# Next block's Q projection and rope tables inside the current attention loop, in a two-layer decoder trunk

## The chip, the cores and the metric

The kernel runs on the eight cores of one Trainium2 chip. Each core computes one of the eight sequences of the batch; the cores exchange nothing. The metric is the device time of the slowest core, in microseconds.

## The reference

Two layers over x of 2048 tokens by 1024 features per core. Each layer first mixes tokens, then runs an MLP:

```python
h = adaln(rms_norm(x, g_mix), sh1, sc1)
q_a,k_a,v_a, q_b,k_b,v_b, gate_a, gate_b = split(h @ w_in)
# A: sliding window 128, 8 query heads, 2 key heads, a learned sink per head
# B: 8 heads, blocks of 256 keys: own block (causal) + the top 3 past blocks by q . mean(k)
q, k = rope(rms_norm(q), positions), rope(rms_norm(k), positions)   # head size 64
y_a = swa_attention(q_a, k_a, v_a, sinks) @ w_o_swa
y_b = moba_attention(q_b, k_b, v_b) @ w_o_moba
x = x + gt1 * ((sigmoid(gate_a) * y_a + sigmoid(gate_b) * y_b) @ w_out)
h = adaln(rms_norm(x, g_mlp), sh2, sc2)
x = x + gt2 * (relu(h @ w_up) ** 2 @ w_down)
```

## The kernel before

Activations are held with features on the partitions. The 2048 tokens are cut into NS = 4 blocks of 512 (index `s`). A small scheduler records every operation in program order with what it reads and writes, derives the semaphores from that, and lets each engine run its own operations in exactly that order. All helpers (`mm`, `act`, `tt`, `ts`, `stt`, `cp`) have one line each, so that in the profile L373 is every matmul, L398 every ScalarE activation, L402, L416 and L428 are VectorE operations, L435 copies.

A layer runs: the keys and values of all tokens (A); then for each block the Q projection, the bias of the block selection, and attention (B0 to B3); then the output projections (C) and the MLP. The change is in B.

- `norm_tile(s, ..., hTs)` normalises block `s` into `hTs`: eight squares on ACT with eight matmuls into one PSUM bank, Ln and Exp, and eight pairs of a DVE operation and an ACT Identity. The bank is the next of `gen_banks`.
- `rope_tables(s)` makes cos and sin of the block: ten DVE operations, then two Sin activations on ACT, which have another activation table than Exp, Ln and Square.
- `qk_item` makes one item (128 of the 1024 Q features) out of three parts. `s0` projects: eight matmuls into `pin`. `s1` squares `pin` on ACT, averages over the head with one matmul into `pm`, runs Ln and Exp on ACT and multiplies `pin` by the result on DVE. `s2` rotates: one matmul into `pr`, and three DVE operations that end in `AT`, which holds Q and later the attention result. `pin` rotates over PSUM banks 0 to 2, `pm` is bank 3, `pr` banks 4 and 5. Two sets of scratch tiles (`qksets`) alternate.
- `run_items` runs eight items in ten steps; step i issues `s0` of item i, then `s1` of item i-1, then `s2` of item i-2. In step 7 `norm_tile(s+1)` stands behind the last projection. `rope_tables(s+1)` follows the ten steps.
- The bias stage works mostly on DVE, with one transpose on PE for each 128 tokens.
- The attention loop runs over `units`. A unit is one tile of 128 keys for up to 512 query columns and has four parts: `score` (matmuls into a score bank `sc`, with a POOL copy of the values and for some units DVE copies of Q), `ex` (one Exp on ACT into a probability tile `pb`), `pv` (one matmul into `po`), and `post`, which for the last unit of a group runs Ln and Exp on ACT and the products on DVE. First come 14 or 16 units of the sliding window (attention A), then eight heads of 4s + 4 units each (attention B, called the MoBA part below): 46, 80, 112 and 144 units for s = 0 to 3. `score` is issued SK = 3 units ahead of `ex` and `pv`, `post` two units behind. Scores rotate over banks 1 to 4, probabilities over four tiles, `po` over banks 5 to 7. For s of 2 and 3 most units have an extra matmul for the bias.

Of the kernel before, what the change touches and what calls it, by code (L numbers as in the profile page):

```python
# [6 lines left out]
F32 = mybir.dt.float32  # L7
BF16 = mybir.dt.bfloat16
# [8 lines left out]
NS = 4  # L17
# [278 lines left out]
def build_program(layers, n_total_layers=2, dbg=None, stop=None):  # L296
    nc = bass.Bass("TRN2", target_bir_lowering=False)
    L = n_total_layers
# [16 lines left out]
    S = Sched()  # L315
    dbg_out = {}
    with ExitStack() as st:
        XA = Arena(nc, st, "XA", 65536, gran=2048)
        AA = Arena(nc, st, "AA", 32768, gran=1024)
        BIG = Arena(nc, st, "BIG", 65536, gran=256)  # L320
# [3 lines left out]
        SF2 = Arena(nc, st, "SF2", 4096, gran=1024)  # L324
# [3 lines left out]
        PS = [PsumBank(nc, st, "ps%d" % i) for i in range(8)]  # L328

        xT = XA.view(0, (8, SEQ), F32)  # L330
        AT = AA.view(0, (8, SEQ), BF16)
# [37 lines left out]
        def mm(out, lhsT, rhs, start, stop):  # L369
            r = list(lhsT.keys) + list(rhs.keys)  # L370
            if not start:
                r += list(out.keys)
            S.add('pe', lambda e, o=out.ap, l=lhsT.ap, rr=rhs.ap: e.matmul(o, l, rr, start=start, stop=stop),  # L373
                  reads=r, writes=out.keys)
# [65 lines left out]
        def memset(out, val, eng='dve'):  # L440
            S.add(eng, lambda e, o=out.ap: e.memset(o, val), writes=out.keys)
# [112 lines left out]
        def GAIN(l, i):  # L554
            return vec(l, 0, 68)[:, 64 + i:65 + i]

        def norm_tile(s, acol, bcol, dest):
            sl = slice(s * 512, (s + 1) * 512)
            bank = psb()
            pm = bank.view(0, (512,), F32)  # L560
            for k in range(8):
                act(dest[:, k], xT[:, k, sl], AF.Square)
                mm(pm, Oones, dest[:, k], start=(k == 0), stop=(k == 7))
            act(rstd, pm, AF.Ln, bias=epsc)
            act(rstd, rstd, AF.Exp, scale=-0.5)
            for k in range(8):
                stt(t1 if k % 2 == 0 else t2, xT[:, k, sl], acol[:, k:k + 1], rstd, ALU.mult, ALU.mult)
                act(dest[:, k], t1 if k % 2 == 0 else t2, AF.Identity, bias=bcol[:, k:k + 1])
# [3 lines left out]
        qkc = [0]  # L572
        pinc = [0]
        qkn = [2]

        def qk_item(proj, gain, dest, cs=None):
            st_ = {}

            def s0():
                st_['pin'] = PS[pinc[0] % 3].view(0, (512,), F32)  # L580
                pinc[0] += 1
                st_['set'] = qksets[qkc[0] % qkn[0]]
                qkc[0] += 1
                proj(st_['pin'])

            def s1():
                sq_, xn_, r_, tt1_ = st_['set']
                pin = st_['pin']
                act(sq_, pin, AF.Square)
                pm = PS[3].view(0, (512,), F32)  # L590
                mm(pm, Bones, sq_, True, True)
                act(r_, pm, AF.Ln, bias=epsc)
                act(r_, r_, AF.Exp, scale=-0.5)
                stt(xn_, pin, gain, r_, ALU.mult, ALU.mult)

            def s2():
                sq_, xn_, r_, tt1_ = st_['set']
                pr = PS[4 + st_.setdefault('prb', qkc[0] % 2)].view(0, (512,), F32)
                mm(pr, Rt, xn_, True, True)
                cos_, sin_ = cs if cs is not None else (cos_s, sin_s)  # L600
                tt(tt1_, xn_, cos_, ALU.mult)
                tt(r_, pr, sin_, ALU.mult)
                tt(dest, tt1_, r_, ALU.add)
            return (s0, s1, s2)

        def run_items(items, fillers=None, after_proj=None, mid=None):
            n = len(items)
            for i in range(n + 2):
                if i == 3 and mid is not None:
                    mid()  # L610
                if fillers:
                    fillers.pop(0)()
                if i < n:
                    items[i][0]()
                if i == n - 1 and after_proj is not None:
                    after_proj()
                if 0 <= i - 1 < n and items[i - 1][1] is not None:
                    items[i - 1][1]()
                if 0 <= i - 2 < n and items[i - 2][2] is not None:
                    items[i - 2][2]()  # L620

        BIGROW = 32768
        AAROW = 16384
# [7 lines left out]
        def layer(l):  # L631
# [112 lines left out]
            biasq3 = SB.view(13312, (8, 8), BF16)  # L744
            E_GS = 1024 // 4
            VECROWF = 1024
            Pb3 = [Pb[0], Pb[1], BIG.view(63744, (512,), BF16), SF2.view(0, (512,), BF16)]
            vaug = [BIG.view(64768 + 256 * i_, (128,), BF16) for i_ in range(3)] + [SB.view(15616, (128,), BF16)]
            for i_ in range(4):
                memset(vaug[i_][:, 64:128], 1.0)  # L750
            norm_tile(0, a1, sh1, hTs)
            rope_tables(0)
            for s in range(NS):
                gen_banks[0] = [6, 7]
                S.mark('L%d B%d qproj' % (l, s))
                sl = slice(s * 512, (s + 1) * 512)
                def mk_q(p):
                    w = wqa if p < 4 else wqb
                    pc = p % 4

                    def proj(pin):
                        for k in range(8):
                            mm(pin, w[:, k, pc * 128:(pc + 1) * 128], hTs[:, k], k == 0, k == 7)
                    return qk_item(proj, GAIN(l, 0 if p < 4 else 2), AT[:, p, sl])
                run_items([mk_q(p) for p in range(8)],
                          after_proj=(lambda s=s: norm_tile(s + 1, a1, sh1, hTs)) if s + 1 < NS else None)
                if s + 1 < NS:
                    rope_tables(s + 1)
                if s == 0:
                    dump('qT0', AT[:, :, 0:512], (128, 8, 512), BF16)  # L770
                if stop == 'Bq':
# [39 lines left out]
                def swa_units(g, tq):  # L811
# [7 lines left out]
                    qrot[0] += 1  # L819
                    qrot[1] += 1  # L820
                    for ci, c in enumerate(chunks):
                        sc = PS[1 + rot['sc'] % 4].view(0, (512,), F32)
                        rot['sc'] += 1
                        pb = Pb3[rot['pb'] % 4]
                        rot['pb'] += 1
                        triap = triL4 if c == i else triU4

# [40 lines left out]
                def moba_units(h):  # L868
# [9 lines left out]
                    for j in range(nch):  # L878
                        cl = j - 4 * s
                        q0 = 0 if cl < 0 else cl * 128  # L880
                        b = j // 2
                        sc = PS[1 + rot['sc'] % 4].view(0, (512,), F32)
                        rot['sc'] += 1
                        pb = Pb3[rot['pb'] % 4]
                        rot['pb'] += 1
                        r = h * 8 + b
                        sel = Raw(identb[:, r:r + 1].ap.to_broadcast([128, 128]), identb.keys)
# [32 lines left out]
                if stop not in ('Bs', 'Bs1', 'Bs2', 'Bs0', 'BsX'):  # L920
                    for h in range(8):
                        moba_units(h)
                SK = 3
                for ui in range(min(SK, len(units))):
                    units[ui][0]()
                for ui in range(len(units) + 2):
                    if ui + SK < len(units):
                        units[ui + SK][0]()
                    if ui < len(units):
                        units[ui][1]()  # L930
                        units[ui][2]()
                    if 0 <= ui - 2 < len(units):
                        units[ui - 2][3]()
                if stop in ('Bs', 'Bm', 'Bs1', 'Bs2', 'Bs0', 'BsX'):
                    return
            gen_banks[0] = [0, 1, 2, 3, 4, 5, 6, 7]
# [169 lines left out]
```

How the kernel before makes its waits and increments, by code:

```python
        def run(engname, eng):  # L105
            waited = {}
            for i in per_eng[engname]:
                op = ops[i]
                need = {}
                for d in op['deps']:
                    p = ops[d]
                    if p['dma_key'] is not None:
                        s, v = dsems[p['dma_key']], p['dmaval']
                    elif needs_edge(op, d):
                        s, v = sems[p['eng']], p['sigval']
                    else:
                        continue
                    kk = id(s)
                    if v > need.get(kk, (None, 0))[1]:
                        need[kk] = (s, v)
                for kk, (s, v) in need.items():
                    if waited.get(kk, 0) >= v:
                        continue
                    eng.wait_ge(s, v)
                    waited[kk] = v
                if op['fn'] is None:
                    continue
                ins = op['fn'](eng)
                if op['dma_key'] is not None:
                    ins.then_inc(dsems[op['dma_key']], 16)
                elif op['signal']:
                    ins.then_inc(sems[engname], 1)
```

## Time and profile before

| | |
|---|---|
| Median of 7 runs | 3439.84 us |
| Device time of the profiled execution | 3439.29 us |
| Its span on the slowest core | 3437.4 us (cores: 3407.8 to 3437.4) |
| PE busy | 2497.8 us, 73% |
| PE weight loads | 1100.7 us, 32% |
| DVE busy | 1489.2 us, 43% |
| ACT busy | 1418.2 us, 41% |
| POOL busy | 286.4 us, 8% |
| Mean granted TensorE clock | 0.84 |
| Part B of layer 0 | about 377 to 1027 us |

Busy shares are means over stages with different limits. The granted clock has two levels, 0.5 (1.2 GHz) and 1.0 (2.4 GHz); a value between them is a mean over a stretch. A matmul of 512 columns that follows another starts 0.2155 us after it at the upper level, though its row shows about 0.38 us from start to end.

### The profile page before, as it was taken

Reading aid. Unit: us, or ns where it says so; the run is one execution under the profiler, and the core shown is the slowest. Engines: PE = TensorE matmul, PEld = TensorE weight load, DVE = VectorE, ACT = ScalarE, POOL = GpSimd, SP = SyncE. Lnnn points to the kernel's source line nnn. Section 1 sums busy time; section 2 is a strip of 40 time slices with the busy share of each in tenths; the row PEclk is TensorE's granted clock in tenths of the full one; section 3 lists DMA queues with packets and bytes.
Section 4 is the critical chain, followed back from the end, with each engine's and each line's share of the span. In section 5 each row is a group of like instructions: output and inputs, shape, how many; then the busy total and the mean of one; then the engine's idle time right before and its main releaser. Section 6 shows DMA issues by size and latency. Waiting matters only on the chain.

```text
span 3437.4 us, 42360 instructions; the slowest of 8 cores (3407.8 to 3437.4 us)
## 1 busy us (share of the span) xinstructions
PE 2497.8 (73%) x11816; PEld 1100.7 (32%) x11816; DVE 1489.2 (43%) x2820; ACT 1418.2 (41%) x2460; POOL 286.4 (8%) x887
## 2 busy tenths in 40 slices
PE   3355545648498987999976554464849998799997
PEld 3122112213143433444432211121314343344444
DVE  1244655352604444444445565535250444444443
ACT  1143455647383344111124445564738334411112
POOL 0100000202040000110000000020204000000000
PEclk6677757769699998999988775776969999899999
DMA  7930000000006040645240000000000504132002
GB/s 154 112 47 1 13 1 1 1 1 1 0 8 92 1 62 13 86 64 86 31 56 1 0 13 1 1 1 0 1 1 10 90 1 72 27 50 37 14 1 98
DMA packets 124463, 107.10 MB, mean 31 GB/s; under 512 B 11216, under 2 KB 119888, under 8 KB 124112
## 3 DMA queue, kind: packets, MB, share of 16 engines
q0 software_dynamic: 118768, 86.42, 17.9%
q1 hardware_dynamic: 5472, 17.98, 1.5%
q8 instruction: 107, 1.75, 0.2%
q14 instruction: 116, 0.95, 0.1%
HBM read 182.41 MB, written 8.39 MB: 56 GB/s over the span
## 4 chain that ended last, share of the span: by engine, by line
PE 57%; DVE 14%; ACT 13%; issue 8%; DMA 6%; DVEq 1%; ACTq 0%; POOL 0%; SPq 0%; POOLq 0%
PE ps L373 56%; ACT SF L398 7%; ACT SB L398 4%; DVE SF L416 3%; DVE SF L402 2%; DVE SF L428 2%; DVE AA L402 2%; DMA AA<-w_in 1%; DMA AA<-w_ada 1%; DMA BIG<-w_o_moba 1%; DMA BIG<-x 1%; DVE BIG L435 1%; ACT AA L398 1%; DVE SB L428 1%; PE ps L377 1%
## 5 line engine op out<-in xcount | busy, mean ns | idle before, releaser
L373 PE MATMUL ps<-SB,BIG 128*128 128x512 bf16 (+2 forms) x5046 | 1241.3, 381 | 150.5 <-ACT SB L398 129.5
L398 ACT ACTIVATE SF<-ps 128x512 f32<-128x512 f32 (+4 forms) x695 | 400.0, 577 | 955.3 <-PE ps L373 944.3
L373 PEld LDWEIGHTS ps<-SB,BIG 128*128 128x128 bf16 x5046 | 503.8, 101 | 770.2 <-issue 265.8
L373 PE MATMUL ps<-AA,BIG 128*128 128x512 bf16 x2560 | 570.4, 380 | 2.7 <-DMA BIG<-w_o_moba 2.7
L373 PE MATMUL ps<-SB,CB 128*128 128x512 bf16 (+1 forms) x688 | 278.0, 414 | 203.6 <-ACT SB L398 162.3
L373 PEld LDWEIGHTS ps<-AA,BIG 128*128 128x128 bf16 x2560 | 249.7, 98 | 303.9 <-issue 7.5
L428 DVE SCALAR_TENSOR_TENSOR XA<-ps,VEC,XA 128x512 f32<-128x512 f32 x320 | 236.4, 750 | 253.6 <-PE ps L373 253.6
L373 PE MATMUL ps<-BIG 128*128 128x512 bf16 (+3 forms) x759 | 245.4, 353 | 109.3 <-ACT BIG L398 77.8
L402 DVE TENSOR_TENSOR AA<-ps,SF 64x128 bf16<-64x128 f32 (+1 forms) x320 | 116.3, 364 | 456.5 <-PE ps L373 235.0
L428 DVE SCALAR_TENSOR_TENSOR SB<-ps,SF 128x512 bf16<-128x512 f32 x256 | 175.9, 691 | 284.1 <-PE ps L373 179.3
L398 ACT ACTIVATE SF<-SF 64x512 f32<-64x512 f32 (+1 forms) x336 | 211.0, 628 | 193.6 <-DVE SF L416 168.1
L428 DVE SCALAR_TENSOR_TENSOR SF<-XA,VEC,SF 128x512 f32<-128x512 f32 x256 | 182.6, 749 | 167.3 <-ACT SF L398 140.3
L398 ACT ACTIVATE SB<-ps 128x512 bf16<-128x512 f32 (+3 forms) x438 | 226.9, 554 | 45.4 <-PE ps L373 40.3
L435 POOL COPY BIG<-BIG 128x64 bf16<-128x64 bf16 x573 | 136.9, 240 | 1021.9 <-PE ps L373 989.1
L398 ACT ACTIVATE SF<-ps,CF 128x512 f32<-128x512 f32 x144 | 99.0, 687 | 260.8 <-PE ps L373 194.8
L402 DVE TENSOR_TENSOR SF<-SF,ps 128x512 f32<-128x512 f32 x128 | 87.9, 687 | 210.6 <-PE ps L373 205.2
L373 PEld LDWEIGHTS ps<-SB,CB 128*128 128x128 bf16 x688 | 69.3, 101 | 333.8 <-issue 300.5
L398 ACT ACTIVATE SB<-SF,VEC 128x512 bf16<-128x512 f32 x192 | 133.8, 722 | 68.2 <-DVE SF L428 68.0
L398 ACT ACT_TABLE_LOAD x46 | 59.0, 1283 | 239.8 <-PE ps L373 120.5
L373 PE MATMUL ps<-SF,CB 128*128 128x512 bf16 x112 | 53.3, 476 | 135.3 <-ACT SF L398 68.4
L373 PEld LDWEIGHTS ps<-BIG 128*128 128x128 bf16 x759 | 81.7, 109 | 217.8 <-issue 184.0
L373 PE MATMUL ps<-AA,SB 128*128 128x512 bf16 (+1 forms) x512 | 99.6, 350 | 41.5 <-ACT BIG L433 19.3
(92 smaller groups left out, 1849.4 us busy)
## 6 DMA issues: line engine op xcount, KB each, us to landing
BIG<-w_up POOLq DMA_DIRECT2D x16, 1024.0 KB, 12.6
BIG<-w_down POOLq DMA_DIRECT2D x16, 1024.0 KB, 22.1
BIG<-w_in POOLq DMA_DIRECT2D x12, 1024.0 KB, 18.2
BIG<-x SPq DMA_DIRECT2D x16, 512.0 KB, 4.0
AA<-w_ada POOLq DMA_DIRECT2D x16, 512.0 KB, 7.4
out<-BIG SPq DMA_DIRECT2D x16, 512.0 KB, 2.7
TAB<-w_ada POOLq DMA_DIRECT2D x12, 512.0 KB, 6.3
SF<-w_ada POOLq DMA_DIRECT2D x12, 512.0 KB, 8.3
```

What stands on the lines that cost most here:

```text
L373: S.add('pe', lambda e, o=out.ap, l=lhsT.ap, rr=rhs.ap: e.matmul(o, l, rr, start=start, stop=stop), reads=r, writes=out.keys)
L377: S.add('pe', lambda e, o=out.ap, i=in_.ap, d=ident.ap: e.transpose(o, i, d), reads=list(in_.keys) + list(ident.keys), writes=out.keys)
L398: S.add('act', lambda e, o=out.ap, i=in_.ap: e.activation(out=o, in_=i, func=func, **kw), reads=r, writes=w)
L402: S.add(eng, lambda e, o=out.ap, a=in0.ap, b=in1.ap: e.tensor_tensor(out=o, in0=a, in1=b, op=op), reads=list(in0.keys) + list(in1.keys), w ...
L416: S.add(eng, lambda e, o=out.ap, a=in0.ap: e.tensor_scalar(out=o, in0=a, scalar1=a1, scalar2=None, op0=op0), reads=r, writes=out.keys)
L428: S.add(eng, lambda e, o=out.ap, x=in0.ap, y=in1.ap: e.scalar_tensor_tensor(out=o, in0=x, scalar=a, in1=y, op0=op0, op1=op1), reads=r, wri ...
L435: S.add(eng, lambda e, o=out.ap, i=in_.ap: e.tensor_copy(out=o, in_=i), reads=in_.keys, writes=out.keys)
```

## The change

`qk_item` takes its banks from a table `qkb` that can be switched. `run_items` becomes `item_steps`, which returns the ten steps as functions instead of running them; with `serial=True` a step issues `s2`, then `s1`, then `s0`. The Q projection of block 0 runs before the loop over blocks, as before. That of block s+1, with its rope tables ahead of it and `norm_tile(s+2)` in its step 7, goes into the attention loop of block s as eleven background steps, one after every third, sixth or ninth unit (s = 0, 1, 2). In the loop the projection has bank 0, and the mean, the rotation and the norm share bank 4. To make room, scores rotate over three banks (1 to 3), probabilities over three tiles, and SK is 2.

```diff
+        qkb = [dict(pin=[0, 1, 2], pm=3, pr=[4, 5])]
             def s0():
-                st_['pin'] = PS[pinc[0] % 3].view(0, (512,), F32)
+                pl = qkb[0]['pin']
+                st_['pin'] = PS[pl[pinc[0] % len(pl)]].view(0, (512,), F32)
+                st_['pmb'] = qkb[0]['pm']
+                prl = qkb[0]['pr']
+                st_['prb'] = prl[pinc[0] % len(prl)]
...
-                pm = PS[3].view(0, (512,), F32)
+                pm = PS[st_['pmb']].view(0, (512,), F32)
...
-                pr = PS[4 + st_.setdefault('prb', qkc[0] % 2)].view(0, (512,), F32)
+                pr = PS[st_['prb']].view(0, (512,), F32)
...
+        def item_steps(items, fillers=None, after_proj=None, mid=None, serial=False):
...
+                if serial:
+                    if 0 <= i - 2 < n and items[i - 2][2] is not None:
+                        items[i - 2][2]()
+                    if 0 <= i - 1 < n and items[i - 1][1] is not None:
+                        items[i - 1][1]()
+                    if i < n:
+                        items[i][0]()
+                    if i == n - 1 and after_proj is not None:
+                        after_proj()
+                    return
...
+            return [(lambda i=i: step(i)) for i in range(n + 2)]
...
-            Pb3 = [Pb[0], Pb[1], BIG.view(63744, (512,), BF16), SF2.view(0, (512,), BF16)]
+            Pb3 = [Pb[0], Pb[1], BIG.view(63744, (512,), BF16)]
...
+            gen_banks[0] = [6, 7]
+            for st__ in q_steps(0):
+                st__()
             for s in range(NS):
...
-                run_items([mk_q(p) for p in range(8)],
-                          after_proj=(lambda s=s: norm_tile(s + 1, a1, sh1, hTs)) if s + 1 < NS else None)
-                if s + 1 < NS:
-                    rope_tables(s + 1)
...
-                        sc = PS[1 + rot['sc'] % 4].view(0, (512,), F32)
+                        sc = PS[1 + rot['sc'] % 3].view(0, (512,), F32)
-                        pb = Pb3[rot['pb'] % 4]
+                        pb = Pb3[rot['pb'] % 3]
...
-                SK = 3
+                bg = []
+                if s + 1 < NS:
+                    qkb[0] = dict(pin=[0], pm=4, pr=[4])
+                    gen_banks[0] = [4]
+                    bg = [lambda s=s: rope_tables(s + 1)] + q_steps(s + 1, serial=True)
+                every = max(1, len(units) // (len(bg) + 1))
+                SK = 2
...
+                    if bg and ui % every == every - 1:
+                        bg.pop(0)()
+                while bg:
+                    bg.pop(0)()
+                qkb[0] = dict(pin=[0, 1, 2], pm=3, pr=[4, 5])
```

## Rows read from the trace of the kernel before

**Rows 1.** Busy time by stretch, layer 0: stretch, length, each engine's busy us, clock.
```profile
524.90:577.80 52.90, 27.93 (x89) 9.09 (x87) 27.58 (x41) 26.95 (x44) 0.41 (x2) 0.73 0.00 0
671.50:722.90 51.40, 26.49 (x93) 8.87 (x92) 27.38 (x41) 26.77 (x44) 0.70 (x4) 0.74 0.00 1
845.80:885.00 39.20, 22.52 (x85) 8.06 (x84) 21.78 (x33) 15.75 (x26) 0.69 (x3) 0.81 0.00 1
787.40:845.80 58.40, 54.31 (x288) 25.95 (x285) 6.33 (x14) 52.52 (x106) 21.50 (x92) 0.97 0.00 1
```

**Rows 2.** The same view, the Q projection of block 1 in layer 1.
```profile
2157.70:2210.70 53.00, 26.86 (x89) 8.63 (x87) 27.49 (x42) 26.76 (x44) 0.41 (x2) 0.73 0.00 1
```

**Rows 3.** Timeline, Q projection of block 1: start, us, engine, line, operation, idle before.
```profile
529.97 0.38 PE L373 MATMUL ps<-SB,CB 128*128 128x512 bf16 x1
530.50 0.69 ACT L398 ACTIVATE SF<-ps,CF 128x512 f32<-128x512 f32 x1 [1.57 <-PE ps L373]
...
540.28 1.89 PE L373 MATMUL ps<-SB,BIG 128*128 128x512 bf16 x8
...
542.01 0.69 ACT L398 ACTIVATE SF<-ps,CF 128x512 f32<-128x512 f32 x1 [2.46 <-PE ps L373]
542.79 0.63 ACT L398 ACTIVATE SF<-SF 128x512 f32<-128x512 f32 x1
543.33 0.58 ACT L398 ACTIVATE SB<-ps 128x512 bf16<-128x512 f32 x1
543.52 0.75 DVE L428 SCALAR_TENSOR_TENSOR SF<-ps,VEC,SF 128x512 bf16<-128x512 f32 x1 [1.61 <-ACT SF L398]
...
544.42 0.38 PE L373 MATMUL ps<-SF,CB 128*128 128x512 bf16 x1
...
544.79 0.68 DVE L402 TENSOR_TENSOR SF<-ps,TAB 128x512 f32<-128x512 f32 x1
...
552.14 4.25 ACT L398 ACTIVATE SB<-XA 128x512 bf16<-128x512 f32 x8
...
565.80 0.58 ACT L398 ACTIVATE SB<-ps 128x512 bf16<-128x512 f32 x1
```

**Rows 4.** Timeline, rope tables behind block 0's projection, and the next table load.
```profile
450.51 0.42 DVE L416 TENSOR_SCALAR SF<-TAB 128x512 f32<-128x512 f32 x1
...
455.53 1.28 ACT L398 ACT_TABLE_LOAD   x1 [9.79 <-DVE TAB L416]
...
456.75 0.11 DVE L441 MEMSET SB<- 128x64 bf16 x1
...
589.52 1.28 ACT L398 ACT_TABLE_LOAD   x1 [4.21 <-PE ps L373]
```

**Rows 5.** Timeline of ACT, MoBA part of block 1, one head to the next.
```profile
649.82 0.61 ACT L398 ACTIVATE BIG<-ps 128x512 bf16<-128x512 f32 x1
...
651.42 0.60 ACT L398 ACTIVATE BIG<-ps 128x512 bf16<-128x512 f32 x1 [0.16 <-PE ps L373]
...
654.83 0.61 ACT L398 ACTIVATE BIG<-ps 128x512 bf16<-128x512 f32 x1
```

**Rows 6.** Timeline, sliding-window part of block 2.
```profile
754.34 1.34 ACT L398 ACTIVATE SF<-SF 64x512 f32<-64x512 f32 x2 [2.98 <-DVE SF L416]
...
755.79 1.23 DVE L402 TENSOR_TENSOR AA<-ps,SF 64x128 bf16<-64x128 f32 x4 [1.54 <-ACT SF L398]
...
759.77 1.34 ACT L398 ACTIVATE SF<-SF 64x512 f32<-64x512 f32 x2 [2.98 <-DVE SF L416]
```

**Rows 7.** Timeline, the last product of block 0's attention.
```profile
526.56 0.69 DVE L402 TENSOR_TENSOR AA<-ps,SF 64x512 bf16<-64x512 f32 x1 [1.75 <-PE ps L373]
```

**Rows 8.** Timeline of PE, MoBA part of block 3, once per head.
```profile
997.43 0.38 PE L373 MATMUL ps<-SB,BIG 128*128 128x512 bf16 x1 [0.63 <-ACT SB L398]
```

**Rows 9.** Busy time by stretch ahead of a fall of the clock, and the matmuls behind it.
```profile
538.70:542.10 3.40, 2.40 (x10) 0.90 (x10) 2.64 (x4) 0.94 (x3) 0.00 (x0) 1.00 0.00 0
542.10:545.50 3.40, 1.52 (x8) 0.61 (x8) 1.95 (x3) 1.71 (x3) 0.00 (x0) 1.00 0.00 0
...
549.26 3.42 PE L373 MATMUL ps<-SB,BIG 128*128 128x512 bf16 x8
```

More of the change, by code:

```diff
@@ L604, in qk_item, with step @@
             return (s0, s1, s2)
-        def run_items(items, fillers=None, after_proj=None, mid=None):
+        def item_steps(items, fillers=None, after_proj=None, mid=None, serial=False):
             n = len(items)
-            for i in range(n + 2):
+            def step(i):
                 if i == 3 and mid is not None:
@@ L620, in run_items @@
                     items[i - 2][2]()
+            return [(lambda i=i: step(i)) for i in range(n + 2)]
+        def run_items(items, fillers=None, after_proj=None, mid=None):
+            for st__ in item_steps(items, fillers, after_proj, mid):
+                st__()
         BIGROW = 32768
@@ L750, in layer, with mk_q, proj, q_steps @@
                 memset(vaug[i_][:, 64:128], 1.0)
+            def mk_q(p, s_):
+                w = wqa if p < 4 else wqb
+                pc = p % 4
+                sl_ = slice(s_ * 512, (s_ + 1) * 512)
+                def proj(pin):
+                    for k in range(8):
+                        mm(pin, w[:, k, pc * 128:(pc + 1) * 128], hTs[:, k], k == 0, k == 7)
+                return qk_item(proj, GAIN(l, 0 if p < 4 else 2), AT[:, p, sl_])
+            def q_steps(s_, serial=False):
+                return item_steps([mk_q(p, s_) for p in range(8)],
+                                  after_proj=(lambda: norm_tile(s_ + 1, a1, sh1, hTs)) if s_ + 1 < NS else None,
+                                  serial=serial)
             norm_tile(0, a1, sh1, hTs)
             rope_tables(0)
+            gen_banks[0] = [6, 7]
+            S.mark('L%d B0 qproj' % l)
+            for st__ in q_steps(0):
+                st__()
             for s in range(NS):
-                gen_banks[0] = [6, 7]
                 S.mark('L%d B%d qproj' % (l, s))
                 sl = slice(s * 512, (s + 1) * 512)
[L757 to L764, printed above, removed]
-                run_items([mk_q(p) for p in range(8)],
-                          after_proj=(lambda s=s: norm_tile(s + 1, a1, sh1, hTs)) if s + 1 < NS else None)
-                if s + 1 < NS:
-                    rope_tables(s + 1)
                 if s == 0:
@@ L881, in moba_units @@
                         b = j // 2
-                        sc = PS[1 + rot['sc'] % 4].view(0, (512,), F32)
+                        sc = PS[1 + rot['sc'] % 3].view(0, (512,), F32)
                         rot['sc'] += 1
-                        pb = Pb3[rot['pb'] % 4]
+                        pb = Pb3[rot['pb'] % 3]
                         rot['pb'] += 1
```

## The prediction

> **What bounds the kernel now.** I read the span and the granted clock of all cores first, then the busy time of each engine by stretch, then the timeline of the stretches that the change touches. The profiled execution spans 3437.4 us and has a device time of 3439.3 us, beside a median of 3439.8 us; the sum below is made against 3439.3. The change lies in the attention part of each layer only (377 to 1027 us in layer 0). In it each block of 512 tokens runs through three stages, and each has another bound.
>
> The Q projection of a block, the three upper lines of [rows 1], holds PE busy for about half of its 51 to 53 us at a mean granted clock of 0.73; DVE and ACT are busy for half of it too. No engine is full: it is a chain that passes from one to the next. In layer 1 the same stage takes the same 53.0 us [rows 2], so I price one layer and double it. The full-causal head attention that I call the MoBA part is another matter. In block 1 ACT begins the fourth exponential of one head at 649.82 and that of the next at 654.83, back to back but for 0.16 us [rows 5]: ACT is full, one 512-wide exponential starting 0.48 to 0.55 us after the other. In block 2 PE is busy 54.3 and ACT 52.5 of 58.4 us at clock 0.97, the last line of [rows 1]: both nearly full. The sliding-window part ahead of it is a cycle of 5.4 us per group, in which DVE waits for ACT (1.54 us before each product) and ACT for DVE (2.98 us before each logarithm) [rows 6]; PE idles there.
>
> **What is removed.** The projection stages of blocks 1, 2 and 3 leave their place: 52.9 + 51.4 + 39.2 = 143.5 us [rows 1]. The three rope tables leave too: DVE goes from 450.51 to 456.75, 6.2 us each, 18.7 in all [rows 4]. With them goes the reload of ACT's table ahead of the first exponential of blocks 0 to 2, 1.28 us each [rows 4], 3.8 in all. Removed per layer: 166.0 us.
>
> **What is added.** The same instructions come back as 11 steps in the loops of blocks 0 to 2, after every third, sixth and ninth unit (46, 80 and 112 units, divided by 12). No instruction is saved. So the question is what one step costs inside a loop whose engines all take their instructions in order. A full step of the new order is: rotate item p-2, normalise item p-1, project item p. It now has one bank for the projection result (0) and one (4) for both the mean and the rotation. I lay it out from the start of the exponential ex(u) at 0, with durations from [rows 3]:
> - ex(u) ends at 0.60; PE takes pv(u) at 0.74 and the rotation matmul at 0.96 (0.38). DVE reads that bank for 0.68 us and is done at 2.10. Only then may the mean matmul write bank 4: 2.24. ACT's square, ready since 1.13, doesn't decide.
> - The logarithm starts 0.53 after the mean matmul (529.97 to 530.50): 2.77. From the start of a logarithm to the next matmul that needs its result are 2.41 us (542.01 to 544.42, over Exp and DVE's multiplication): 5.18. That multiplication reads bank 0, so the eight projection matmuls can't start before it ends.
> - They take 1.7 us to issue; then comes the score of unit u+3, and its exponential can start at about 7.4.
> Two exponentials, u+1 and u+2, run from 4.15 on because their scores are ready; that is all the cover there is. Undisturbed, ex(u+3) would start at 3 x 0.545 = 1.64. A full step costs 7.4 - 1.64 = 5.8 us, on ACT and on PE alike. Bounds: the 1.9 us of ACT's own three operations if all waits were covered, and 7.7 if the eight matmuls run at 1.2 GHz. I take 5.8, because every link has its row.
>
> The other steps in the same way. Step 1 (nothing to rotate) 4.8. Step 8 (nothing to project) 7.4 less the projection: 3.6. Step 9 0.3. Step 0, only eight matmuls, 1.9 in MoBA and nothing in the sliding-window part, where PE's wait hides it. Step 7 of blocks 0 and 1 also holds the norm of the next tile: from its first square to the next free ACT slot 13.7 us pass (552.14 to 565.80, the last two lines of [rows 3]), and the next exponential stands behind all of it on ACT; first square at 5.5, so 19.2 - 0.54 = 18.6. In the sliding-window part a step overlaps what DVE does anyway: 4.2. The rope tables fall there in all three blocks: DVE's 6.2 us lengthen the cycle, while ACT's two table loads (1.28 each) and two sines lie beside the 2.7 us of DVE work that follows: 6.2. Bounds 3.6 (DVE idles 1.5 of 5.4) and 8.8 (the whole chain with both loads).
>
> Block 0: 6.2 + 0 + 2 x 4.2 + 4 x 5.8 + 18.6 + 3.6 + 0.3 = 60.3. Block 1: 6.2 + 0 + 4.8 + 5 x 5.8 + 18.6 + 3.6 + 0.3 = 62.5. Block 2: 6.2 + 1.9 + 4.8 + 6 x 5.8 + 3.6 + 0.3 = 51.6. The tail of an attention loop also becomes visible: before, the projection started at 524.9 under the last head's logarithm, exponential and product, which end at 527.2 [rows 7]; now the bias stage's DVE work stands behind that product: 2.3 us, three times, 7. Added per layer: 181.4 us. Net +15.4 per layer, **+31 us**.
>
> **One score fewer in flight.** Score and probability tiles go from four to three and the lead from three units to two. While ACT runs a head's Ln and Exp (about 1.3 us), PE lives on its backlog. In block 3 it already runs dry for 0.63 us once per head [rows 8]. One unit less is 0.65 us less backlog (three matmuls at 0.2155). Where ACT is the full engine (blocks 0 and 1) this costs nothing; in blocks 2 and 3, 16 heads a layer, 0 to 0.65 us each. I take 0.5, near the upper end, since the idle time is there already: 8 a layer, **+16 us**.
>
> **The clock.** In the projection stage the granted clock was 1.0 over 3.4 us in which PE was busy 2.4, again over 3.4 us in which it was busy 1.5, and then fell to the 1.2 GHz level, where the eight matmuls took 3.42 us instead of 1.89 [rows 3, 9]. A full step leaves PE with two matmuls in 4.2 us, less than what stood ahead of that fall. So the projection in the step should often run at 1.2 GHz: +1.5, and +0.4 for the two single matmuls. There are 5 + 7 + 8 = 20 such steps per layer in MoBA. Never and always give 0 and 38 us a layer; at two in three it is 25 a layer, **+51 us**. I take that because the activity in a step is below that of the row, but the level follows with a delay that may spare some.
>
> Sum: 3439.3 + 31 + 16 + 51 = **3537 us**.
>
> The row shows that the mean matmul and the rotation each wait for another engine's read. The Trainium skill (Perfetto Trace Analysis, Matmuls) says that independent matmul groups should rotate through different PSUM banks so that the evacuation of one overlaps the next; the change does the reverse for the projection. By that rule the added steps keep their stalls, which is the forecast.
>
> **The rivals.**
> - *The steps are absorbed (faster).* If exponentials in flight covered every wait of a MoBA step, it would cost ACT's own 0.58 + 0.69 + 0.63 = 1.9 us. That is 3.9 less for 15 full steps and 2.9 less for two steps 1: 64 a layer, with the clock held: 3439 + 31 + 16 - 129 = 3357 us. It decides from the point where a full step costs less than 5.8 - (15.4 + 8)/15 = 4.2 us. Against it: only two scores are in flight, 1.1 us of cover for a chain of 5 [rows 3, 5]. For it: PE and ACT both have half of the projection stage idle [rows 1]. The Trainium skill (Perfetto Trace Analysis, Optimization Strategy) says that where the most contended engine changes over time, interleaving those regimes may help; by that rule the time would be this one.
> - *Only the chain counts.* The clock holds and the shorter lead is free: 3439 + 31 = 3470 us. For it: the clock held 1.0 through most of MoBA [rows 1].
> - *The low clock spreads.* After a step the units between steps stay at 1.2 GHz too. Block 2's MoBA, PE-bound at 0.97, would take about 1.8 times its 58.4 us: +47 a layer, 3537 + 94 = 3631 us. Against it: 6 to 9 dense units follow each step.
> - *No difference.* Small misses in 5.8 and 18.6 cancel the sum: a time within 7 us of before.
>
> **How the numbers follow.** Forecast 0.48, chain only 0.20, absorbed 0.14, clock spreads 0.12, no difference 0.06. About 0.2% is what a measurement can tell from no change. Slower by more: 0.80; within: 0.06; faster: 0.14. The range runs from 3435, which takes in chain only and no difference, to 3630; it leaves out the absorbed case and half of the case above.
>
> **What would show it.** In the profile after: MoBA stretches in which, once every 3, 6 or 9 units, PE has a gap of about 2.4 us ahead of the eight projection matmuls, put down to DVE, and ACT one of about 2 us behind the two covered exponentials; the mean matmul waiting for DVE; one gap of 13 us or more per block 0 and 1 at the norm; the eight matmuls at 3.4 us where the clock is at its lower level; per-head PE idle of 1.1 in block 3 against 0.63. The attention part of a layer should be 40 to 60 us longer. I am wrong if the projection matmuls in the loop have no gap ahead of them, or if a full step costs under 4.2 us.

## The result, and the profile of the changed kernel

| | before | changed |
|---|---|---|
| Time where nothing disturbs the chip | 3439.8 us | about 3594 us |
| Ratio (95% interval) | | 1.0446 (1.0425 to 1.0466) |
| Profiled execution | 3439.3 us | 3589.9 us |
| Span of its slowest core | 3437.4 us | 3588.0 us |

The 3439.8 is a median. The ratio times it is 3593.3; 3594 is used below, as in the expectations. Single executions of the changed kernel lie between 3579 and 3616 us (median 3589.5, mean 3592.9), and those in which one half of the chip ran slower for another reason are left out. So a difference against 3594 is good to 4 or 5 us. The kernel became slower, as forecast, and by 154 us instead of 98: beyond the forecast of 3537, inside its range (3435 to 3630).

The page of the changed kernel, its first lines: the number of instructions of each engine is that of before, and their busy time, but for PE's, is within 16 us of it (weight loads within 20). PE's grew by 74 us because the same matmuls take longer at the lower clock.

```profile
span 3588.0 us, 42194 instructions; the slowest of 8 cores (3553.2 to 3588.0 us)
PE 2572.2 (72%) x11816; PEld 1121.0 (31%) x11816; DVE 1497.9 (42%) x2820; ACT 1433.9 (40%) x2460; POOL 290.4 (8%) x887
```

The busy time by stretch, kernel before: the four MoBA parts of layer 0, each from its first to its last exponential (stretch, length, busy us of PE, PE's weight loads, DVE, ACT and POOL, granted clock).

```profile
499.58:524.19 24.61, 14.34 (x86) 7.45 (x86) 9.79 (x26) 21.02 (x47) 6.82 (x30) 0.83 0.00 1
628.06:670.98 42.92, 29.48 (x153) 13.57 (x153) 10.16 (x26) 37.60 (x79) 14.12 (x60) 0.89 0.01 1
781.42:845.30 63.88, 55.90 (x294) 26.64 (x294) 10.15 (x26) 56.01 (x112) 21.53 (x92) 0.97 0.00 1
938.96:1023.98 85.02, 76.70 (x390) 35.85 (x390) 10.15 (x26) 74.95 (x143) 29.21 (x124) 0.98 0.01 1
```

The same view of the changed kernel, and in the last two lines what is left between the loops of blocks 0 and 1 and of blocks 1 and 2.

```profile
508.49:593.56 85.07, 43.79 (x155) 17.55 (x153) 33.48 (x59) 43.78 (x84) 7.98 (x32) 0.62 0.00 0
648.20:760.43 112.23, 65.34 (x235) 24.13 (x235) 38.45 (x66) 64.88 (x122) 15.05 (x61) 0.76 0.00 1
823.57:951.42 127.85, 91.53 (x377) 37.38 (x376) 32.48 (x58) 72.33 (x135) 22.55 (x93) 0.85 0.00 1
1008.29:1099.25 90.96, 80.55 (x392) 35.63 (x392) 10.15 (x26) 77.45 (x143) 29.44 (x125) 0.95 0.00 1
593.56:602.37 8.81, 3.00 (x12) 1.20 (x13) 4.00 (x21) 1.49 (x5) 0.41 (x2) 0.68 0.00 1
760.43:777.35 16.92, 4.41 (x29) 2.05 (x29) 8.08 (x40) 1.50 (x5) 0.89 (x4) 0.61 0.00 0
```

The stages of [rows 1] are gone from between the loops, where 55 to 73 us have become 9 to 19. In their place the MoBA parts of blocks 0 to 2 grew by 60, 69 and 64 us. Take block 1: ACT was busy 37.6 of 42.9 us before, and is busy 64.9 of 112.2 now. It was the full engine, and it now waits 47 us. Block 3, which has no steps, grew too, by 5.9 us; the first experiment below, which has the shorter lead and no steps, shows the same 5.9.

One step of the new order in the middle of block 1's MoBA part, changed kernel, timeline (start, us, engine, line, operation, idle before and who ended it):

```profile
684.54 0.59 ACT L398 ACTIVATE SB<-ps 128x512 bf16<-128x512 f32 x1
...
685.60 0.38 PE L373 MATMUL ps<-SB,CB 128*128 128x512 bf16 x1
...
686.08 0.69 DVE L402 TENSOR_TENSOR SF<-ps,TAB 128x512 f32<-128x512 f32 x1 [0.41 <-PE ps L373]
...
686.92 0.38 PE L373 MATMUL ps<-SF,CB 128*128 128x512 bf16 x1 [0.94 <-DVE SF L402]
687.39 0.69 ACT L398 ACTIVATE SF<-ps,CF 128x512 f32<-128x512 f32 x1 [1.77 <-PE ps L373]
688.17 0.63 ACT L398 ACTIVATE SF<-SF 128x512 f32<-128x512 f32 x1
688.71 0.58 ACT L398 ACTIVATE SB<-ps 128x512 bf16<-128x512 f32 x1
688.90 0.75 DVE L428 SCALAR_TENSOR_TENSOR SF<-ps,VEC,SF 128x512 bf16<-128x512 f32 x1 [1.33 <-ACT SF L398]
689.18 0.48 ACT L398 ACTIVATE BIG<-ps 128x384 bf16<-128x384 f32 x1
...
689.80 3.57 PE L373 MATMUL ps<-SB,BIG 128*128 128x512 bf16 x8 [2.51 <-DVE SF L428]
...
693.79 0.38 ACT L398 ACTIVATE SB<-ps 128x256 bf16<-128x256 f32 x1 [4.12 <-PE ps L373]
```

Read from the exponential at 684.54, the forecast's offsets stand beside it: the mean matmul at 2.38 (2.24 forecast), the logarithm at 2.85 (2.77), the first projection matmul at 5.26 (5.18). Two exponentials run in the shadow, at 688.71 and 689.18. The third starts at 9.25, where 7.4 was forecast for the upper clock; the row of the eight matmuls is 3.57 us long, where that of [rows 3] at the upper level is 1.89. From the first start to the last they took 2.9 us, against 1.5 at the upper level. Of the 20 such groups in layer 0's MoBA parts 13 took 2.9 us, one took 1.5, and the others lie between.

### The profile page after: what moved, and what is told of

It is laid out like the page before. It is cut to its first block, busy times and chain, and to the rows that moved or that the text cites. A ratio compares the mean times of both kernels' runs of the same rounds, so it can differ in the third digit from the quotient of the medians.

```text
span 3588.0 us, 42194 instructions; the slowest of 8 cores (3553.2 to 3588.0 us)
## 1 busy us (share of the span) xinstructions
PE 2572.2 (72%) x11816; PEld 1121.0 (31%) x11816; DVE 1497.9 (42%) x2820; ACT 1433.9 (40%) x2460; POOL 290.4 (8%) x887
## 4 chain that ended last, share of the span: by engine, by line
PE 58%; DVE 15%; ACT 13%; issue 7%; DMA 6%; DVEq 0%; ACTq 0%; POOL 0%; SPq 0%; POOLq 0%
PE ps L373 57%; ACT SF L398 7%; ACT SB L398 4%; DVE SF L428 2%; DVE SF L416 2%; DVE AA L402 2%; DVE SF L402 2%; DMA AA<-w_ada 1%; DMA BIG<-w_o_moba 1%; DVE SB L428 1%; DMA BIG<-x 1%; DVE BIG L435 1%; DMA AA<-w_in 1%; ACT AA L398 1%; ACT L398 1%
## 5 line engine op out<-in xcount | busy, mean ns | idle before, releaser
L373 PE MATMUL ps<-SB,BIG 128*128 128x512 bf16 (+2 forms) x5046 | 1309.5, 397 | 254.4 <-ACT SB L398 100.3
L373 PEld LDWEIGHTS ps<-SB,BIG 128*128 128x128 bf16 x5046 | 514.4, 103 | 929.9 <-issue 457.8
L398 ACT ACTIVATE SF<-ps 128x512 f32<-128x512 f32 (+2 forms) x504 | 298.9, 596 | 951.5 <-PE ps L373 946.9
L398 ACT ACTIVATE SB<-ps 128x512 bf16<-128x512 f32 (+3 forms) x566 | 299.7, 545 | 201.7 <-PE ps L373 194.1
L373 PE MATMUL ps<-BIG 128*128 128x512 bf16 (+3 forms) x759 | 253.5, 364 | 144.9 <-DVE BIG L435 123.0
L435 POOL COPY BIG<-BIG 128x64 bf16<-128x64 bf16 x573 | 140.9, 247 | 1096.8 <-PE ps L373 1067.0
L398 ACT ACTIVATE BIG<-ps 128x512 bf16<-128x512 f32 (+1 forms) x254 | 138.4, 545 | 87.8 <-PE ps L373 83.3
L373 PE MATMUL ps<-CB 128*128 128x128 bf16 (+1 forms) x380 | 133.7, 352 | 0.0
```

Source lines behind the costliest of these rows:

```text
L398: S.add('act', lambda e, o=out.ap, i=in_.ap: e.activation(out=o, in_=i, func=func, **kw), reads=r, writes=w)
L435: S.add(eng, lambda e, o=out.ap, i=in_.ap: e.tensor_copy(out=o, in_=i), reads=in_.keys, writes=out.keys)
```

## The experiments

Steps are compared in one way throughout. Every unit has one exponential, so the time from the exponential behind which a step stands to that behind which the next step stands can be taken in two kernels, and the difference is what the step costs. The kernel to compare with is the first experiment, which has the shorter lead and no steps. "Between loops" is the time from one block's last exponential to the next block's first.

The experiments ran in three sessions, in which the kernel before took 3440.7, 3445.2 and 3446.0 us. Ratios are to the kernel before of the same session. Times from different sessions can differ by 5 us for that reason alone: the first, the rotation bank, the two projection banks and the held clock are of the first session, the lead alone, the early copies and the first spread kernel of the second, the other three of the third.

### The shorter lead alone

The kernel before with the room given away and nothing put into it.

```diff
-                        sc = PS[1 + rot['sc'] % 4].view(0, (512,), F32)
+                        sc = PS[1 + rot['sc'] % 3].view(0, (512,), F32)
-                        pb = Pb3[rot['pb'] % 4]
+                        pb = Pb3[rot['pb'] % 3]
-                SK = 3
+                SK = 2
```

> The kernel before with three score banks, three probability tiles and a lead of two units, nothing interleaved. Theory: ACT's Ln and Exp at the end of a head let PE run dry one unit earlier, about 0.8 us per head in blocks 2 and 3 (32 heads over both layers), nothing in blocks 0 and 1: 3440 + 25 = 3465 us. Rival: the shorter lead is free by itself and costs only beside the steps: 3440 us. Second rival: it also lengthens the sliding-window cycle: over 3480 us.

Measured: 3498.9 us, ratio 1.0168 (1.0151 to 1.0186): 58 us where the forecast had 16, and more than this run's own 3465. By part, layer 0: MoBA of block 0 took 36.0 instead of 24.6 us, of block 1 45.2 instead of 42.9, of block 2 68.8 instead of 63.9, of block 3 90.9 instead of 85.0; some 27 us a layer. The rival that the sliding-window cycle gets longer explains little: its four parts together grew by 2.5 us. Blocks 2 and 3 cost 0.6 to 0.7 us per head, near the 0.5 of the forecast. Block 0, where nothing was forecast, costs most. Who PE waits for there, first the kernel before, then this one (waits of PE: us in total, times, longest; the windows 504:527 and 504:545 begin some 5 us inside the part and end 3 and 10 us behind it):

```profile
PE ps L373 <- ACT SB L398: 9.2, 7, 2.3
```
```profile
PE ps L373 <- DVE SB L435: 9.7, 4, 4.3
PE ps L373 <- DVE BIG L435: 6.0, 3, 2.2
PE ps L373 <- ACT SB L398: 1.5, 1, 1.5
```

L435 on DVE is the copy of Q that the first score of a head needs. Its place in the short-lead kernel, timeline of DVE and PE:

```profile
513.45 0.69 DVE L402 TENSOR_TENSOR AA<-ps,SF 64x512 bf16<-64x512 f32 x1 [3.64 <-ACT SF L398]
...
514.05 0.28 DVE L435 COPY SB<-AA 64x512 bf16<-64x512 bf16 x1
...
514.48 0.38 PE L373 MATMUL ps<-SB,BIG 128*128 128x512 bf16 x1 [1.81 <-DVE SB L435]
```

In block 0 a head has four units. The order follows from the kernel's loop. With a lead of three, the copy for a head's first unit is issued in the same iteration as the closing product two heads earlier, and ahead of it. With a lead of two it comes one iteration later, behind that product; the product waits for ACT's logarithm and exponential, the copy waits behind the product on DVE, and PE behind the copy. Once per head PE has run out of work.

### Only the lead, and only the copy

Two kernels tell the lead from the buffers and from the copy's place. One sets `SK = 2` and keeps four score banks and four probability tiles. The other is the first experiment with the Q copies taken out of `score` and issued one unit ahead of it:

```diff
                 SK = 2
+                for ui in range(SK + 1):
+                    units[ui][4]()
...
+                    if ui + SK + 1 < len(units):
+                        units[ui + SK + 1][4]()
```

> The kernel before with a lead of two units and nothing else: still four score banks and four probability tiles. Theory: the lead alone makes the loss, banks and tiles are free: 3499 us as in e1_short_lead. Rival (the third bank or the fourth tile is what is missed): clearly less, 3440 to 3470 us.

> e1_short_lead with one edit: DVE's copies of Q for a group's or head's first unit are issued one unit ahead of its score, so that they stand on DVE ahead of the product that closes the head before last. Theory (with a lead of two, the copy falls behind that product, which waits for ACT's Ln and Exp; PE waits for the copy): the 11 us that block 0's MoBA part gained in each layer go, those of blocks 2 and 3 (5 to 6 each) stay: 3499 - 25 = 3474 us. Rival (the loss in block 0 is the backlog of scores, as in blocks 2 and 3): no change, 3499 us.

Measured: 3499.8 us with the lead alone, ratio 1.0141 (1.0099 to 1.0184), with the same parts as above (36.4 us for block 0's MoBA part). Its interval overlaps that of the first experiment, so the buffers cost nothing that these runs can tell; the lead does. With the early copies 3479.3 us, 1.0089 (1.0066 to 1.0113), and block 0's MoBA part is back at 26.6 us. PE's waits there, of the kernel with early copies (window 504:530):

```profile
PE ps L373 <- ACT SB L398: 6.1, 5, 1.5
PE ps L373 <- ACT BIG L398: 4.7, 3, 3.0
```

DVE is gone from the list. So 20 of the 58 us are the copy's place in DVE's queue (27 by the ratios). By part it is 9.4 of the 11.4 us of block 0; block 1 keeps its 2.2. What remains besides, 6.4 us in block 2 and 6.3 in block 3 per layer, comes with the smaller backlog: PE's wait at each change of head in block 3 was 0.61 to 0.75 us before and is 0.94 to 1.12 here. That is about half a microsecond per head, and the part grew by 0.8; the rest was not taken apart.

The same edit on the changed kernel:

> The changed kernel with DVE's copies of Q issued one unit earlier, as in e5_early_copy. Theory (the shorter lead puts them behind waits of DVE in the changed kernel too, there also behind the steps' operations): at least the 20 us of e5_early_copy, 3594 - 25 = 3569 us. Rival (the steps' own waits hide the copies): 3590 us or more.

Measured: 3573.3 us, 1.0370 (1.0355 to 1.0386), some 21 us less than the changed kernel (26 by the ratios, 15 between the two profiled executions). Without the steps the same edit gave 20, 27 and 18. So the two causes add up, within what these runs can tell.

### The rotation in a bank of its own

The changed kernel, with bank 7 for the rotation and `po` on banks 5 and 6 (the `post` of one unit of block 0 goes one place earlier for that).

```diff
-                    po = PS[5 + rot['po'] % 3].view(0, (512,), F32)
+                    po = PS[5 + rot['po'] % 2].view(0, (512,), F32)
-                    qkb[0] = dict(pin=[0], pm=4, pr=[4])
+                    qkb[0] = dict(pin=[0], pm=4, pr=[7])
```

> The changed kernel, but the rotation matmul writes bank 7, which attention results give up (they rotate over banks 5 and 6). The mean matmul no longer waits for DVE's read of the rotation. Theory of the chain: it starts at 1.27 instead of 2.24 us after the exponential in about 42 steps: 3594 - 40 = 3554 us. Rival (the level of the clock decides, and a shorter gap changes nothing for it): the same 1.0 us is still gained, but not more; if the chain isn't what binds, 3594 us.

Measured: 3511.1 us, 1.0204 (1.0186 to 1.0222), 83 us less than the changed kernel. Over the 15 full MoBA steps of layer 0 a step costs 5.4 us on average, where it costs 7.1 in the changed kernel. The chain became shorter by DVE's read, 1.0 us by the expectation, and the clock gained with it: 7 of the 20 projections took 2.9 us from first start to last, where it was 13. How the 1.7 us divide between the two was not measured. Below stand one of its projections in the timeline, and the MoBA parts of blocks 1 and 2 by stretch (granted clock 0.76 and 0.85 without the edit):

```profile
662.72 2.52 PE L373 MATMUL ps<-SB,BIG 128*128 128x512 bf16 x8 [2.56 <-DVE SB L428]
```
```profile
636.76:734.98 98.22, 59.34 (x235) 23.26 (x235) 38.33 (x66) 64.79 (x121) 15.50 (x61) 0.79 0.00 1
798.12:913.82 115.70, 86.85 (x377) 36.05 (x376) 32.30 (x58) 72.31 (x136) 22.26 (x93) 0.89 0.00 1
```

### Two banks for the projection

Bank 7 goes to `pin` instead, and a step issues normalise, project, rotate. The projection no longer waits for DVE's multiplication of the item before, and it gives PE work while ACT takes the logarithm. The `po` edit is that of the kernel above.

```diff
+                    if 0 <= i - 1 < n and items[i - 1][1] is not None:
+                        items[i - 1][1]()
+                    if i < n:
+                        items[i][0]()
                     if 0 <= i - 2 < n and items[i - 2][2] is not None:
                         items[i - 2][2]()
...
+                    qkb[0] = dict(pin=[0, 7], pm=4, pr=[4])
```

> The changed kernel with two banks (0 and 7) for the projection result in the loop, attention results over banks 5 and 6, and each step in the order normalise item p-1, project item p, rotate item p-2. The projection then waits for nothing and the mean matmul only for ACT's square. Theory (a step costs the chain that PE and ACT both wait for): a full step costs ACT's 1.9 us and the wait for the mean matmul, 2.8 us in all instead of 8.3; norm and rope tables as before: 3594 - 206 = 3388 us, faster than the kernel before. Rival (ACT and PE have no room in the MoBA part whatever the order): a step still costs 5 us or more, over 3470 us.

Measured: 3467.8 us, 1.0081 (1.0064 to 1.0099): 126 us less than the changed kernel, and faster than the short lead alone. It missed its own 3388, because a full step costs 3.8 us on average and not 2.8: 2.0 to 4.2 in block 2, but 2.5 to 5.8 in block 1 and 2.0 to 6.4 in block 0. Block 2 shows what is gained when no gap stands ahead of the projection:

```profile
803.17 1.89 PE L373 MATMUL ps<-SB,BIG 128*128 128x512 bf16 x8
```
```profile
791.54:884.08 92.54, 78.18 (x377) 34.09 (x376) 31.54 (x58) 71.93 (x136) 23.87 (x93) 0.95 0.00 1
```

These two kernels answer the forecast's remark on banks: the mean and the rotation in one bank cost 83 us of 3594; the projection in one bank, together with the order of issue that went with it, cost 126. The order alone, with one bank, was not run. The 126 also holds what the first kernel shows, since here the mean matmul no longer stands behind DVE's read of the rotation either. The Trainium skill (Perfetto Trace Analysis, Matmuls) says that independent matmul groups should rotate through different PSUM banks; the runs agree.

### The clock held up

The changed kernel, with nine matmuls behind each mean matmul in the loop whose result is not used (bank 7, with the same `po` edit as above). The chain is left as it is; PE's idle time behind the mean matmul is filled.

```diff
+                if qkb[0]['pin'] == [0]:
+                    fb = PS[7].view(0, (512,), F32)
+                    for _f in range(9):
+                        mm(fb, Bones, Raw(sq_.ap), True, True)
```

> The changed kernel with nine added 512-column matmuls (their result is not used, they write bank 7, which attention results give up) behind each mean matmul in the loop, where PE waits 2.9 us for Ln, Exp and DVE. Theory of the clock: the eight projection matmuls then run at 2.4 GHz (1.5 from the first start to the last instead of 2.9) and so do the units behind them: about 2 us less in 40 steps, 3594 - 80 = 3514 us. Rival (the low level costs little, the chain is all): the added matmuls fit in the gap or overrun it, 3594 to 3640 us.

Measured: 3538.5 us, 1.0279 (1.0254 to 1.0303): 56 us less with 432 matmuls more, against the 80 expected. Mean and filling are the group of ten here, the projection behind it takes 1.89 us, and the parts of blocks 1 and 2 have the clock at 0.87 and 0.95.

```profile
848.09 2.32 PE L373 MATMUL ps<-SB,CB 128*128 128x512 bf16 x10 [0.94 <-DVE SF L402]
...
850.97 1.89 PE L373 MATMUL ps<-SB,BIG 128*128 128x512 bf16 x8 [0.56 <-DVE SB L428]
```
```profile
646.05:749.00 102.95, 71.11 (x307) 27.89 (x307) 38.23 (x66) 64.00 (x122) 15.32 (x61) 0.87 0.00 1
811.94:928.90 116.96, 95.63 (x449) 41.06 (x448) 32.47 (x58) 72.47 (x135) 22.17 (x93) 0.95 0.00 1
```

The 15 full MoBA steps now cost 5.8 us on average, and none of the 20 projections took more than 2.3 us from first start to last (15 took 1.5). That is the forecast's chain at the upper clock; the other 1.3 us of the 7.1 are the clock.

### The parts spread over the loop

Back to four score banks (1, 2, 3 and 7) and a lead of three, with `po` on banks 5 and 6. The rope tables and the norm of the next block go piece by piece into the `post` of the sliding-window units, where DVE and ACT wait for each other. An item's projection, square, mean, Ln with Exp, and rotation go behind different units, so that nothing waits at once for what was just issued. `fin` is Ln, Exp and DVE's multiplication. The slots of one item, which starts at slot `b`. Items follow every three slots in block 0 and every four in blocks 1 and 2, and a slot is a unit, in block 2 two units. The first line is that of block 0; elsewhere the projection is cut in two halves in slots `b` and `b + 1`:

```diff
+                    slots[b][1].append(lambda h=h: h(0, 8))
+                    slots[b + period - 2][1].append(square)
+                    slots[b + period - 1][0].append(mean)
+                    slots[b + period - 1][1].append(fin)
+                    slots[b + period][1].append(rotate)
```

> The same Q projections, norms and rope tables inside the attention loops, but cut small. Norm and rope tables of the next block lie in the eight closing parts of the sliding-window groups, ACT's pieces where it waits for DVE and DVE's where it waits for ACT. In the MoBA part an item goes as projection, square, mean matmul, Ln and Exp with the multiplication, rotation, each behind another unit, so that none of them is waited for. Lead of three and four score banks (bank 7 among them, attention results over 5 and 6), three probability tiles. Theory (the loss of the change is waits of the chain, not work): an item costs ACT's 1.9 us or PE's ten matmuls of 0.2155, norm and rope tables nearly nothing: per layer 180 removed, 5 + 62 + 7 added, 3440 - 212 = 3228 us. Rival (the MoBA part has no room): items cost 5 us each as in e4_two_pins, 3440 - 212 + 140 = 3370 us or more.

Measured: 3396.1 us, 0.9840 (0.9798 to 0.9881). Faster than before, though far from the expected 3228. The sliding-window parts took 39.4, 40.0 and 40.0 us against 36.1, 37.2 and 37.4 before: norm and tables together cost 3 us a block there. As steps they had cost about 19: 7 for the tables and 12 for the norm (the 19 of step 7 less the 7 of a full step). The items still cost 5.5 to 6 us each: block 0's MoBA part took 71.4 us against 24.6, eight items in 46.8. In block 1 ACT waits for PE (window 605:685):

```profile
ACT SB L398 <- PE ps L373: 15.8, 5, 4.0
ACT SF L398 <- PE ps L373: 15.7, 8, 4.2
```

A second kernel spaces the items five slots apart in blocks 1 and 2 and issues the Q copies two units earlier.

> e7_spread with five units per item instead of four in blocks 1 and 2 (one left free between projection and square) and DVE's copies of Q two units earlier. Theory (what items still cost, 5.6 to 6 us each, is ACT waiting for the projection and PE for a copy behind DVE's multiplication): about 1.5 us less per item in two blocks and two layers, 3396 - 45 = 3350 us. Rival (the MoBA part has room for no more than this): 3390 us or more.

Measured: 3371.0 (the profiled execution), 3372.7 and 3421.2 us, ratio 0.9832 (0.9757 to 0.9907). Its MoBA parts took 65.6, 79.0 and 101.5 us against 71.4, 90.7 and 108.0. The interval is too wide to part it from the kernel before it, or to decide between the 3350 of its theory and the 3390 of its rival.

### Only the filling of the sliding window

Last, the norm and the tables in the sliding-window part as above, and the Q projection back between the loops with its three banks; four score banks, lead three, three probability tiles.

```diff
+                if s > 0:
+                    for st__ in q_steps(s):
+                        st__()
...
+                                if fill is not None and fill[0]:
+                                    for f_ in fill[0].pop(0):
+                                        f_()
```

> Only the norm and the rope tables of the next block go into the attention loop, into the closing parts of its sliding-window groups as in e7_spread. The Q projection stands between the loops as before, with its banks, four score banks, a lead of three, three attention result banks; probability tiles are three, since the fourth is scratch here. Theory (the sliding-window part has idle ACT and DVE time, the MoBA part has none): per layer 3 x 13.7 of norm and 22.4 of rope tables and reloads go, 3 x 3.3 come: 3440 - 107 = 3333 us. Rival (the three probability tiles cost the MoBA parts what the short lead did, or the norm in the projection stage was covered): 3380 us or more.

Measured: 3361.1 us, **0.9750 (0.9730 to 0.9769)**, the fastest of all. The stretches: sliding window and MoBA of block 0, the way between the loops, MoBA of block 1.

```profile
439.72:479.08 39.36, 21.45 (x95) 9.48 (x93) 31.54 (x95) 28.55 (x47) 3.71 (x14) 0.63 0.00 1
479.08:505.43 26.35, 14.24 (x86) 7.41 (x86) 11.21 (x28) 24.13 (x51) 6.74 (x30) 0.82 0.00 1
505.43:551.95 46.52, 25.62 (x92) 9.18 (x93) 25.03 (x53) 16.01 (x29) 0.41 (x2) 0.76 0.00 1
592.67:638.00 45.33, 30.33 (x154) 13.71 (x154) 11.57 (x28) 41.15 (x84) 14.11 (x60) 0.87 0.01 1
```

Without norm and tables the way between the loops takes 46.5 us instead of 66.6, and the sliding window gives up 3.3 for it. Left outside, the eight items cost about 39 us a block (the third stage of [rows 1], which has no norm); inside they cost 46.8 even when spread. It missed its 3333 by 28 (by 21 if the ratio is taken): the MoBA parts of blocks 0 to 2 are 1.8, 2.4 and 2.7 us longer than before, which no run took apart.

The two kernels bear on the forecast's rival by the Trainium skill (Perfetto Trace Analysis, Optimization Strategy), which says that where the most contended engine changes over time, interleaving those regimes may help. In these runs it did where DVE and ACT of the receiving stage waited for each other; in the MoBA parts, where ACT or both ACT and PE were nearly full, the items cost more than outside.

## Why the prediction was right, and where it was short

Per layer, in us; the steps' sum is that of layer 0, by the comparison with the short-lead kernel.

| Term | forecast | measured |
|---|---|---|
| Removed, less the tails (166.0 - 7) | -159 | -158 |
| Steps, clock included (174.4 + 25) | +199 | +204 |
| Shorter lead | +8 | +27 |
| Net, twice | +98 | +146 (of 154) |

- *What bounds the kernel.* Right. ACT went from nearly full to waiting 47 of 112 us in block 1, and no instruction was saved. The attention part of a layer grew by 75 us, where 40 to 60 were named as the sign.
- *Removed.* Right in sum: 151 us less between the loops and some 8 ahead of block 0's first exponential.
- *The full step, 5.8 us at the upper clock.* Right: 5.8 on average where the clock was held, and every link within 0.15 us in the step shown. The gap ahead of the projection is 2.51 us (2.4 forecast). Some of the agreement is luck: single steps cost 3.9 to 8.5 us, and the mean with the clock is 6.1 in block 0, 7.1 in block 1 and 7.8 in block 2, where one price, 7.05, was forecast for all. The point from which the change pays was put at 4.2. The two-bank kernel goes under it, at 3.8, and is 31 us faster than the short lead alone, but not faster than before: with 27 us a layer for the lead instead of 8 the same formula gives 3.0.
- *The clock.* Right in size: two in three steps at the lower level were forecast, 1.3 us a step; 13 of 20 projections ran at it throughout, and 7.1 less 5.8 is 1.3. Holding it gave back 56 us, where 51 were forecast.
- *The norm in step 7.* Right: 19.1 and 19.6 us against 18.6. In block 1 the first square starts at 724.33 and the next exponential at 737.99, 13.7 us later, as forecast:

```profile
724.33 4.26 ACT L398 ACTIVATE SB<-XA 128x512 bf16<-128x512 f32 x8 [1.68 <-PE ps L373]
...
737.74 0.59 PE L373 MATMUL ps<-SB,BIG 128*128 128x512 bf16 x1 [8.62 <-DVE SB L435]
```

- *The rope tables.* 7.1 to 7.6 us against 6.2. The term left out what is queued behind the ten operations: they delay the Q copies as well, so PE waits for the last of them and the copy, and DVE's cycle starts late again.

```profile
467.94 0.69 DVE L428 SCALAR_TENSOR_TENSOR TAB<-SF,TAB 128x512 f32<-128x512 f32 x1
...
468.55 0.18 DVE L435 COPY BIG<-AA 64x128 bf16<-64x128 bf16 x1
...
468.88 0.27 PE L373 MATMUL ps<-BIG 128*128 128x128 bf16 x1 [8.34 <-DVE BIG L435]
```

- *Step 8* was 4.3 to 6.7 us, not 3.6, and step 1 in block 1 6.5, not 4.8. The steps in the sliding window were 3.0 and 4.5 against 4.2, and step 0 there cost 0 in block 1 and 0.8 in block 0; in block 2 it cost 0.6, not 1.9. The misses nearly cancel: the sum, 204, is nearer to its 199 than its terms are.
- *The shorter lead* is the step that failed: "Where ACT is the full engine (blocks 0 and 1) this costs nothing". It was priced as a backlog of matmuls, by which the idle time of PE in block 3 came out right: 1.11 us at the change of head, where 1.1 was forecast. The part's cost, 0.7 us a head, came out above the 0.5.

```profile
1037.41 0.38 PE L373 MATMUL ps<-SB,BIG 128*128 128x512 bf16 x1 [1.11 <-ACT SB L398]
```

  But a lead is also a place in every queue that `score` issues to. One unit less moved the Q copy behind the closing product, and with heads of four units that product is recent. Block 0 cost 11.4 us a layer, 9.4 of them by the copy; block 1 cost 2.3, which the early copies did not give back and no run explains. The forecast had asked for the queues that a moved step passes, and did not ask it of the lead.
- *The rivals.* Absorbed steps: the full step would have had to cost 1.9 us; it cost 7.1. Chain only (3470): ruled out by the held clock, 56 us faster, and by the short lead, 58 us slower. Low clock between the steps too (3631): block 2's MoBA part would have run at the lower level throughout; its granted clock is 0.85. In the seven stretches between its eight projections, each from the end of one to the next step, it is 1.00 four times, and 0.94, 0.82 and 0.80. Two of them:

```profile
853.90:859.80 5.90, 4.78 (x22) 2.26 (x21) 0.82 (x2) 4.00 (x8) 1.42 (x6) 0.80 0.00 0
883.90:888.10 4.20, 4.20 (x23) 2.00 (x22) 0.00 (x0) 3.44 (x7) 1.32 (x6) 1.00 0.00 0
```

The last 8 us of the 154 have two sources. The steps' sum begins at the first step; taken as whole parts, the loops of blocks 0 to 2 grew by 207 and not 204, and layer 0's attention, with its earlier first exponential, ends 75.3 us later. Twice that is 150.6, the whole difference between the two profiled executions. The other 3 to 4 us are what that execution of the changed kernel lies below the 3594. The parts are read on one core of one execution each.

## What to carry over

Before a stage is put into another's loop, write out one step as a chain over the in-order queues: what it costs is the length of the chain less what is in flight, here 7 us for 1.9 us of ACT work, and what it leaves PE idle comes back as a lower clock. Put such work where both of its engines wait on each other, in pieces that depend on nothing just issued; norm and tables cost 3 us there and about 19 as steps. When a lead or a buffer count is cut, look at every queue that the leading part issues to, not only at the engine that is to be kept fed.

## What the runs showed that was not expected

- Matmuls whose results nobody uses made the kernel faster: nine behind each mean matmul, 3594 to 3538 us, with the projection's row at 1.89 us instead of up to 3.57.
- Taking DVE's read of the rotation out of the chain (a bank of its own) gained 83 us, about twice the 40 expected; the granted clock was also higher, 0.89 against 0.85 in block 2's MoBA part.
- A lead of two instead of three units costs 1.4% (1.0099 to 1.0184) with every buffer still there. A third to a half of that is one copy of 0.28 us per head that came to stand behind a product instead of ahead of it.
